# An encoder step's first stage: shorter start-up pieces taken pairwise, spare accumulators, and a later row norm

## The reference: what is computed

```python
def macaron_half(x, g, w_in, w_out):
    a, b = jnp.split(rms_norm(x, g) @ w_in, 2, axis=-1)
    return x + 0.5 * ((jax.nn.silu(a) * b) @ w_out)
```

## Time and profile before

| | us |
|---|---|
| median of 3 runs | 1278.88 |
| lowest and highest | 1278.86 and 1279.47 |
| the profiled execution | 1280.21 |
| its span | 1278.4 |
| PE busy in the span | 1265.4 |
| DVE busy | 741.6 |
| ACT busy | 561.2 |

### The profile page before, as it was taken

The page is one execution under the profiler, slowest core; times in us unless marked ns, Lnnn a source line. Parts: engine busy times, 40 slices in busy tenths (PEclk is TensorE's granted clock), DMA queues, the critical chain, the costliest instruction groups (busy, mean ns, idle before and its releaser), DMA issues.

```text
span 1278.4 us, 22446 instructions
## 1 busy us (share of the span) xinstructions
PE 1265.4 (99%) x8784; PEld 1243.9 (97%) x8784; DVE 741.6 (58%) x1128; ACT 561.2 (44%) x827; POOL 174.8 (14%) x208
## 2 busy tenths in 40 slices
PE   9999999999999999999999999999999999999999
PEld 8999999999998999999999999999997899999999
DVE  7756574555677656554454675554446756656433
ACT  7534363353275533333343453433345763343322
POOL 0300020046143100000122000000124510000000
PEclk9999999999999999999999999999999999999999
DMA  8454445553203444444443533454451144343443
GB/s 279 163 160 150 161 139 174 195 188 132 100 34 130 164 151 145 160 163 139 151 164 123 196 133 138 157 164 160 135 187 34 55 144 159 137 164 131 135 140 128
DMA packets 39661, 187.45 MB, mean 147 GB/s; under 512 B 4369, under 2 KB 14353, under 8 KB 24497
## 3 DMA queue, kind: packets, MB, share of 16 engines
q1 hardware_dynamic: 38272, 183.38, 41.8%
q0 software_dynamic: 1184, 3.13, 1.1%
q10 hardware_dynamic: 144, 0.11, 0.0%
HBM read 179.70 MB, written 6.90 MB: 146 GB/s over the span
## 4 chain that ended last, share of the span: by engine, by line
PE 95%; DVE 2%; ACT 1%; issue 1%; DMA 1%; SPq 0%; ACTq 0%; DVEq 0%
PE bank L490 29%; PE bank L492 29%; PE bank L491 29%; PE bank L752 1%; PE bank L713 1%; PE bank L890 1%; PE bank L755 1%; PE bank L722 1%; DVE wlo L1526 1%; DMA raw<-in_w_ffn_in 1%; ACT whi L1120 0%; PE outs L516 0%; ACT ew L1281 0%; PE outs L518 0%; PE outs L500 0%
## 5 line engine op out<-in xcount | busy, mean ns | idle before, releaser
L490 PE MATMUL bank<-xhi,whi 128*128 128x320 f32 (+1 forms) x1760 | 545.8, 310 | 3.0 <-DVE wlo L1901 1.1
L492 PE MATMUL bank<-xhi,wlo 128*128 128x320 f32 (+1 forms) x1760 | 543.0, 309 | 0.0
L491 PE MATMUL bank<-xlo,whi 128*128 128x320 f32 (+1 forms) x1760 | 543.0, 309 | 0.0
L1526 DVE TENSOR_TENSOR wlo<-raw,whi 128x2048 fp32r<-128x2048 f32 (+1 forms) x177 | 364.1, 2057 | 230.2 <-ACT whi L1120 230.1
L1120 ACT ACTIVATE whi<-raw 128x2048 fp32r<-128x2048 f32 (+1 forms) x177 | 304.1, 1718 | 242.3 <-PE bank L492 237.9
L490 PEld LDWEIGHTS bank<-xhi,whi 128*128 128x128 f32 x1760 | 330.5, 188 | 6.2 <-issue 3.4
L491 PEld LDWEIGHTS bank<-xlo,whi 128*128 128x128 f32 x1760 | 330.6, 188 | 0.5
L492 PEld LDWEIGHTS bank<-xhi,wlo 128*128 128x128 f32 x1760 | 330.5, 188 | 0.0
L490 PE MATMUL bank<-hhi,whi 128*128 128x320 f32 x704 | 219.0, 311 | 0.0
L492 PE MATMUL bank<-hhi,wlo 128*128 128x320 f32 x704 | 217.5, 309 | 0.0
L491 PE MATMUL bank<-hlo,whi 128*128 128x320 f32 x704 | 217.5, 309 | 0.0
(11 more groups left out here) (233 smaller groups left out, 1041.5 us busy)
## 6 DMA issues: line engine op xcount, KB each, us to landing
raw<-in_w_ffn_in SPq DMA_DIRECT2D x86, 1024.0 KB, 4.8
raw<-in_w_ffn_out SPq DMA_DIRECT2D x64, 704.0 KB, 4.2
raw<-in_w_in_a SPq DMA_DIRECT2D x10, 1024.0 KB, 4.8
raw<-in_w_out SPq DMA_DIRECT2D x8, 1024.0 KB, 4.9
raw<-in_w_kv SPq DMA_DIRECT2D x6, 1024.0 KB, 4.8
raw<-in_w_mkv SPq DMA_DIRECT2D x4, 1024.0 KB, 4.7
raw<-in_w_in_b SPq DMA_DIRECT2D x4, 1024.0 KB, 4.7
raw<-in_w_ffn_in SPq DMA_DIRECT2D x8, 256.0 KB, 7.2
```

Of the source, the lines that this page charges most:

```text
L490: mm(acc, wh, mhi(ks[q]), start=start and q == 0, stop=False)
L491: mm(acc, wh, mlo(ks[q]), start=False, stop=False)
L492: last = mm(acc, wl, mhi(ks[q]), start=False, stop=stop and q == nk - 1)
L1526: tt(wlo[slot][:, 0:size], raw[slot][:, 0:size], f32(whi[slot][:, 0:size]), ALU.subtract).then_inc(lo_ready[slot], 1)
```

## The change

In the code this is in one place, the stage `in0` and what feeds it:

- the inputs `xT` and `memT` are laid out on the host with the partition first, so that a partition's two tiles of x are one row of 2560 bytes instead of two of 1280, and the memory is rows of 8 KB instead of 1 KB;
- the four pieces are taken pairwise: x, `raw[0]` and `raw[1]` of piece q are loaded, split and multiplied before piece q+1. The first piece of `raw[1]` is issued by ACT, behind `early`; the others by SP behind the same piece of `raw[0]`;
- the squares and their sums come after all pieces on ACT and DVE;
- pair 1's slot 0 is loaded in two halves, the first as soon as the first two pieces of slot 0 are split, and is split in two halves; both of these and pair 1's slot 1 are split ahead of the row norm on ACT and DVE;
- pair 1's tiles 0 and 1 go to `banks[4]` and `banks[5]` and don't wait for `acc_free`;
- PE's `row_norm` moves behind pair 1's tile 0, `biases` behind its tile 3 and into the accumulator `HS`;
- ACT's `settle` waits for `early` instead of the constants; POOL issues the loads of the constants after pair 1's slot 0 has landed.

```diff
+START = [(0, 2), (2, 4), (4, 6), (6, 8)]
+LAST = len(START) - 1
...
-            x_v = a["xT"].rearrange("(k p) r -> p k r", p=P)
-            for q in range(4):
-                sp.dma_start(x[:, 2 * q:2 * q + 2], x_v[:, 2 * q:2 * q + 2]).then_inc(d_x[q], 16)
...
-            load_stage("in0", 1, 2)
...
+            x_v = a["xT"]
+            for q, (k0, k1) in enumerate(START):
+                own = slice(256 * k0, 256 * k1)
+                sp.dma_start(x[:, k0:k1], x_v[:, k0:k1]).then_inc(d_x[q], 16)
+                sp.dma_start(raw[0][:, own], weights["in0"][0][:, own]
+                             ).then_inc(d_piece[q] if q < LAST else landed[0], 16)
+
+                if q:
+                    sp.dma_start(raw[1][:, own], weights["in0"][1][:, own]
+                                 ).then_inc(d_piece1[q] if q < LAST else landed[1], 16)
+
+            sp.wait_ge(piece_lo, 2)
+            sp.dma_start(raw[0][:, 0:BLK // 2], weights["in0"][2][:, 0:BLK // 2]).then_inc(d_third, 16)
+            sp.wait_ge(lo_ready[0], 1)
+            sp.dma_start(raw[0][:, BLK // 2:BLK], weights["in0"][2][:, BLK // 2:BLK]).then_inc(landed[0], 16)
+            sp.wait_ge(lo_ready[1], 1)
+            sp.dma_start(raw[1][:], weights["in0"][3]).then_inc(landed[1], 16)
+            sp.dma_start(memt[:], a["memT"]).then_inc(d_mem, 16)
...
+                    for q, (k0, k1) in enumerate(START):
+                        pe.wait_ge(xn_lo, k1)
+                        for slot, some in ((0, piece_lo), (1, piece1_lo)):
...
+                            if slot == 0 and k1 == KD // 2:
+                                last.then_inc(first_half, 1)
...
-                        wait_acc(t0 + 4 * i + j)
+
+                        spare = halves and j < 2
+                        if not spare:
+                            wait_acc(t0 + 4 * i + j)
...
-                        product(banks[j][:, 0:R], slot, col, 256, range(KD), KD,
+                        product(banks[4 + j if spare else j][:, 0:R], slot, col, 256, range(KD), KD,
...
-                    body(1, False, lambda j: stats() if j == 1 else None, halves=True)
+                    body(1, False, lambda j: row_norm(stage, R) if j == 0 else stats() if j == 3 else None, halves=True)
...
             act.dma_start(early[:], a["early"]).then_inc(d_early, 16)
+            act.dma_start(raw[1][:, 0:512], weights["in0"][1][:, 0:512]).then_inc(d_piece1[0], 16)
...
+            for k in range(KD):
+                nc.scalar.activation(sq8[:, k, :], x[:, k, :], ACT.Square).then_inc(sq_ready, 1)
+
+            act.wait_ge(d_third, 16)
+            act.wait_ge(first_half, 1)
+            nc.scalar.activation(whi[0][:, 0:BLK // 2], raw[0][:, 0:BLK // 2], ACT.Copy).then_inc(third_hi, 1)
             act.wait_ge(landed[0], 16 * (PAIR0["in0"] + 1) + 16)
             act.wait_ge(acc_ready, TILE0["in0"] + 2)
-            nc.scalar.activation(whi[0][:, 0:BLK // 2], raw[0][:, 0:BLK // 2], ACT.Copy).then_inc(third_hi, 1)
+            nc.scalar.activation(whi[0][:, BLK // 2:BLK], raw[0][:, BLK // 2:BLK], ACT.Copy).then_inc(hi_ready[0], 1)
+            split_hi(1, PAIR0["in0"] + 1, BLK, acc_ready, TILE0["in0"] + 4)
             row_norm("in0", R)
-            nc.scalar.activation(whi[0][:, BLK // 2:BLK], raw[0][:, BLK // 2:BLK], ACT.Copy).then_inc(hi_ready[0], 1)
...
+            dve.wait_ge(hi_ready[0], PAIR0["in0"] + 2)
+            tt(wlo[0][:, BLK // 2:BLK], raw[0][:, BLK // 2:BLK], f32(whi[0][:, BLK // 2:BLK]), ALU.subtract
+               ).then_inc(lo_ready[0], 1)
+            split_lo(1, PAIR0["in0"] + 1, BLK)
             row_norm("in0", R)
...
-    o["memT"] = a["mem_prompt"][0].T
+
+    xT = np.concatenate([a["x_prompt"][0].T, a["x_sample"][0].T], axis=1)
+    o["xT"] = xT.reshape(KD, P, R).transpose(1, 0, 2)
+    o["memT"] = a["mem_prompt"][0].T.reshape(KD, P, N_MEM).transpose(1, 0, 2)
```

More of the change, by code:

```diff
@@ L364, in encoder_kernel @@
         d_early = sem("d_early")
-        d_x = [sem(f"d_x{q}") for q in range(4)]
+        d_x = [sem(f"d_x{q}") for q in range(LAST + 1)]
         d_const = sem("d_const")
@@ L587, in first_pieces @@
                 def first_pieces():
[L589 to L595, removed]
+                    for q, (k0, k1) in enumerate(START):
+                        pe.wait_ge(xn_lo, k1)
+                        for slot, some in ((0, piece_lo), (1, piece1_lo)):
+                            if q == LAST:
+                                pe.wait_ge(lo_ready[slot], 1)
+                            else:
+                                pe.wait_ge(some, q + 1)
                             for col in range(2):
@@ L966, in biases @@
                 pe.wait_ge(d_const, CONST)
-                mm(banks[4][0:H_A, 0:NREL + 1], table[:], hot[:], start=True, stop=True).then_inc(trel_ready, 1)
+                mm(HS[0:H_A, 0:NREL + 1], table[:], hot[:], start=True, stop=True).then_inc(trel_ready, 1)
             def stats_mkv0(j):
@@ L1111, in settle @@
             def settle():
[L1114 removed]
+                act.wait_ge(d_early, 16)
             def split_hi(slot, n, size, used_sem, used):
@@ L1212, in body @@
                     for c in range(2):
-                        if c == 1:
+                        if c == 1 and not (stage == "in0" and isinstance(i, int) and i == 0):
                             split_hi(1, n0 + i + 1, BLK if size is None else size, acc_ready, t0 + 4 * i + 4)
@@ L1403, in _ @@
                     input_hi(x[:, k, :], xhi[:, k, :], "ffn1_0", k)
[L1404 to L1422, removed]
+                act.wait_ge(d_piece[q] if q < LAST else landed[0], 16)
@@ new lines, in _ @@
+                nc.scalar.activation(whi[0][:, own], raw[0][:, own], ACT.Copy
+                                     ).then_inc(piece_hi if q < LAST else hi_ready[0], 1)
+                act.wait_ge(d_piece1[q] if q < LAST else landed[1], 16)
+                nc.scalar.activation(whi[1][:, own], raw[1][:, own], ACT.Copy
+                                     ).then_inc(piece1_hi if q < LAST else hi_ready[1], 1)
+            for k in range(KD):
+                nc.scalar.activation(sq8[:, k, :], x[:, k, :], ACT.Square).then_inc(sq_ready, 1)
@@ L1640, in body @@
                 def body(i, size, at=None):
+                    spare = stage == "in0" and isinstance(i, int) and i == 1
                     for c in range(2):
                         dve.wait_ge(acc_ready, t0 + 4 * i + c + 1)
-                        tt(gate[:, c, :], banks[c][:, 0:R], r[:], ALU.mult).then_inc(acc_free, 1)
+                        tt(gate[:, c, :], banks[4 + c if spare else c][:, 0:R], r[:], ALU.mult).then_inc(acc_free, 1)
                         if at:
@@ L1663, in ffn_in @@
                     for i in range(3):
-                        body(i, BLK, third if stage == "in0" and i == 0 else None)
+                        body(i, BLK)
                         after(i)
@@ L1894, in _ @@
             nc.vector.memset(f32(lf8_lo[:]), 0.0)
-            for q in range(4):
-                inputs_lo("in0", "ffn1_0", lambda k: x[:, k, :], R, tiles=(2 * q, 2 * q + 1))
-                if q < 3:
+            for q, (k0, k1) in enumerate(START):
+                own = slice(256 * k0, 256 * k1)
+                inputs_lo("in0", "ffn1_0", lambda k: x[:, k, :], R, tiles=range(k0, k1))
+                if q < LAST:
                     dve.wait_ge(piece_hi, q + 1)
@@ L1900, in _ @@
                     dve.wait_ge(hi_ready[0], 1)
[L1901 to L1913, removed]
+                tt(wlo[0][:, own], raw[0][:, own], f32(whi[0][:, own]), ALU.subtract
+                   ).then_inc(piece_lo if q < LAST else lo_ready[0], 1)
+                if q < LAST:
                     dve.wait_ge(piece1_hi, q + 1)
@@ L1916, in piece1 @@
                     dve.wait_ge(hi_ready[1], 1)
[L1917 to L1925, removed]
+                tt(wlo[1][:, own], raw[1][:, own], f32(whi[1][:, own]), ALU.subtract
+                   ).then_inc(piece1_lo if q < LAST else lo_ready[1], 1)
+            for k in range(1, KD):
+                dve.wait_ge(sq_ready, k + 1)
+                if k >= 2:
+                    dve.wait_ge(ssum_step, k)
+                tt(ssum[:], sq8[:, 0, :] if k == 1 else ssum[:], sq8[:, k, :], ALU.add
+                   ).then_inc(ssum_step, 2 if k == 1 else 1)
             dve.wait_ge(third_hi, 1)
```

31 lines of the change are left out of this document (11 added, 20 removed).

## The result

| | before | after |
|---|---|---|
| median, us | 1279.13 (5 runs) | 1285.96 (5 runs) |
| lowest and highest | 1278.86 and 1279.47 | 1284.95 and 1287.31 |
| the profiled execution | 1280.21 | 1285.31 |
| its span | 1278.4 | 1283.5 |
| mean granted clock of the executions | 1.0 | 0.996 to 0.999 |

The change made the kernel slower: the ratio is 1.0055, with a 95% interval from 1.0043 to 1.0068. The forecast was 1281.9 with a range from 1280.3 to 1283.3. The direction was right, the size less than half of what came.

The account below looks back on a forecast made before the run. PE bounds the kernel, through when pair 2's first tile starts. Row norm +5.7 (wait removal, -1.4, included), chain -3.2 and first product +0.5 make +3.0 us: 1283.2 for the profiled execution, 1281.9 on the median, range 1280.3 to 1283.3.

Parts of the forecast that it names:

- What bounds the kernel: PE, fed without a gap from pair 2's first tile (38.91 us): whatever moves that tile moves the end as much.
- The row norm and the chain behind it: Row norm +5.7 us later; chain from it to pair 2's first tile 16.5 us instead of 19.7, -3.2 us.
- The new wait ahead of pair 1's third tile: PE waits 0.7 us for three results to be taken from the banks; costs nothing by itself.
- The first product: Start of PE's products: 256 KB more on ACT's queue delay it, taken as +0.5 us between -0.5 and +0.85.
- the longer rows: Rival at the start: first product 0.5 us early, time 1280.9; low end of the main case, no separate chance.
- The estimate of +0.85: First product late by the full +0.85 us if the piece on ACT's queue takes its share from x; time 1282.2.
- The pairwise pieces, -1.4 us: PE's wait for slot 0's second piece disappears, as it is needed after 24 matmuls instead of 12: -1.4 us.
- the step to the median: Profiled execution 1.3 us over the median of 1278.88; the difference put on the median turns 1283.2 into 1281.9.
- The clock: Rival: PE's 3.6 us stand ahead of pair 2 lowers its clock, 2.6 us on top, 1284.5; chance 8%.
- The sum: Pair 2's first tile: 5.7 - 3.2 + 0.5 = +3.0 us, at 41.9 instead of 38.9; time 1281.9 us.

Follow-up runs that it names:

- fill: Changed kernel with 20 matmuls on constants between biases and pair 2's first tile, keeping PE busy while it waits: 1283.62 us, ratio 1.0037.
- norm_early: Changed kernel with PE's row norm put back ahead of pair 1: 1283.67 us, ratio 1.004.
- mem_later: Changed kernel with the three portions of memory work one pair later on ACT and DVE: 1280.49 us, ratio 1.0011.
- a_sp: Changed kernel with slot 1's first piece issued by SP behind slot 0's instead of by ACT: 1284.65 us, ratio 1.004.
- both_sp: Changed kernel with row norm ahead of pair 1, memory work one pair later and slot 1's first piece issued by SP: 1279.44 us, ratio 0.9999.
- b_layouts: Kernel before with only the new layouts of x and of the memory: 1279.35 us, ratio 1.0000.
- before_look3: Kernel before, unchanged, a further single execution: span 1277.1 us, time 1278.90 us.
- fill_warm: Changed kernel with 20 matmuls on constants ahead of pair 2 and 23 instead of 19 at the start: 1283.56 us, ratio 1.0031.
- b_extra8: Kernel before with eight more subtractions behind the eight memlo on DVE, lengthening PE's wait ahead of pair 2: 1284.54 us, ratio 1.0043.
- b_extra4: Kernel before with four more subtractions behind the eight memlo on DVE: 1281.77 us, ratio 1.0016.
- both_warm: Changed kernel with row norm ahead of pair 1, memory work one pair later and 23 instead of 19 start matmuls: 1278.92 us, ratio 0.9993.

## Why the prediction was right or wrong, point by point

- *What bounds the kernel:* right. Pair 2's first tile is followed by 1239.4 to 1239.8 us in every profiled execution without a fall of the clock behind it, and fill ends where that says (41.92 and 1281.4).
- *The row norm and the chain behind it:* right. L513 stands at 25.38 (25.4 forecast). From it to pair 2's first tile it is 16.5 us, the sum's 16.5. The new wait ahead of pair 1's third tile has 0.57 us of idle time, 0.73 with the restart (0.7 forecast). norm_early and mem_later move the tile as the terms say.
- *The first product:* +0.5 was right for the profiled execution (7.71 against 7.20). Its reason was right too, its size too small: the seven traces in which ACT issues the piece have the first product at 7.62 to 7.94, the two in which SP does (a_sp, both_sp) at 6.68 and 6.79. So the piece costs about 1.0 us, and the 7.20 was itself late. That the longer rows could give back 0.7 us is not borne out: b_layouts shows no gain, with an interval too wide to exclude one of half a microsecond. The estimate of +0.85, which the text had made by the Trainium skill ("DMA: Bandwidth & Descriptors", Specifications and Queues, rings and completion order) and set aside as undecided, was the nearer one.
- *The pairwise pieces, -1.4 us, and the step to the median:* this step failed. The trace had the wait of 1.4 us, but the execution of typical length has only 0.4 us of idle time there, and the shortest none. The text noticed that the profiled execution stands 1.3 us over the median of 1278.88, and then took these 1.3 us off the changed kernel as well, 1283.2 to 1281.9. It should have asked where they lie. They lie ahead of the second piece, in the wait that the change removes and in the first product that it sets anew, so the changed kernel does not have them: before_look3, which took 1278.90 us, has pair 2's first tile at 37.55 instead of 38.91. Without that step the sum gives 1283.2; fill and fill_warm measured 1283.62 and 1283.56. Against the median of the larger batches (tile at 38.0) the sum is +3.9, and fill and fill_warm measured +4.4 and +4.1.
- *The clock:* the rival was priced well (2.6 us, 2.3 measured between fill and the changed kernel, 2.1 by the spans) and its condition was the forecast's own 3.6 us, but it was given 8% and left out of the sum. Every execution of the changed kernel has a mean clock below 1.0. This was the larger of the two errors. The text went by the longest stall of the start, 1.1 us, and had no row for one three times as long; it should have held the chance near even.
- *The sum:* 4.1 to 4.4 us of position and 2.3 to 2.4 of clock make 6.4 to 6.8 of the 6.8 measured. The changed kernel's two longest executions, 1287.1 and 1287.31 us, fit a fall at the start as in mem_later (mean clock 0.996 instead of 0.997), but no trace of that kernel shows one.

## What to carry to other kernels

When the profiled execution is longer than the median, find out which wait makes it so before crediting its removal: a wait that varies from run to run is worth its typical length, not that of the one trace. A stall on the critical engine is priced with what it may do to that engine's clock. If the forecast's own case holds a stand far longer than any whose effect a trace shows, the fall belongs in the case with a weight of its own, not at the edge. Work that may come late (here the memory's preparation) should not stand in a queue ahead of what a chain to the bound engine needs.

## What the runs showed of the hardware

In the traces TensorE's granted clock fell to 0.50, the 1.2 GHz level, with stands of PE of 3.72 us (after), 3.73 (a_sp), 3.63 (b_extra8) and 3.12 (norm_early). It did not with one of 2.04 us (b_extra4) or where 20 matmuls on constants left 0.60 us (fill). The stand's length alone does not tell when: in after the clock fell about 1.6 us into the stand, in b_extra8 about 0.7 us after its end. At the start a stand of 1.93 us was enough (mem_later), and one of 1.54 in both_warm was not. The clock stayed low for 3.4 us (b_extra8, norm_early, a_sp, mem_later) or 6.8 us (after). By the spans the first cost 1.4 to 1.6 us, the second 2.1. A matmul of 128x320 started 0.267 us after the one before at that level and 0.147 at the full clock.

The granted clock read 1.00 from the span's start in every trace, although the first 19 matmuls took up to 0.285 us each (before): a clock that has not risen yet has to be read from the matmuls' step.

A transfer on ACT's queue delayed those of SP's queue beside it: 256 KB cost the first product 1.0 us (a_sp).
